# Gathering the rows of two expert tables alternately, head by head, in a fused two-block kernel

## The reference, cut to what matters

```python
def block(args):                 # 128 tokens: xb (128,1024), eb, gb (128,8,16)
    xb, eb, gb = args
    ub = u_tab[eb]
    act = _gelu(jnp.einsum('td,thkd->thk', xb, ub)) * gb
    vb = v_tab[eb]
    return jnp.einsum('thk,thkd->td', act, vb)
```

## Time and profile before

| what | value |
|---|---|
| median of three executions | 3803.32 us (3788.68 to 3813.45) |
| profiled execution: its own time | 3798.31 us |
| its span in the profile | 3796.5 us |
| TensorE clock granted, mean | 0.851 of full |
| first gather issued, last gather issued | 161.3 us, 1983.2 us |
| PE / VectorE / ScalarE / GpSimd busy | 70% / 54% / 21% / 49% of the span |

### The profile page before, as it was taken

One profiled execution on the slowest core, in us unless ns is written; L12 is line 12 of the kernel. 1 busy time (PEld: TensorE's weight loads), 2 busy tenths in 40 slices (PEclk: granted clock), 3 DMA queues, 4 the chain that ended last, 5 costly groups with the idle time before them and its releaser, 6 DMA issues.

```text
span 3796.5 us, 37057 instructions
## 1 busy us (share of the span) xinstructions
PE 2674.6 (70%) x14128; PEld 1994.0 (53%) x14128; DVE 2038.2 (54%) x4133; ACT 802.5 (21%) x1515; POOL 1860.8 (49%) x1389
## 2 busy tenths in 40 slices
PE   6521887207862277542776888888889998998999
PEld 3421444004431144211224777777789997777887
DVE  6599867888678877588443534544220103532010
ACT  2100111001110011111113322332332322443231
POOL 0166656775567756488761322222354543125463
PEclk8755999558886599776998987998999999999999
DMA  5388889897899879999991210000223332012332
GB/s 173 138 310 299 288 276 338 306 341 261 298 314 344 314 264 333 343 336 336 353 345 28 67 28 1 1 1 1 56 73 91 88 90 59 26 45 78 95 95 78
DMA packets 417970, 693.79 MB, mean 183 GB/s; under 512 B 35784, under 2 KB 280691, under 8 KB 417667
## 3 DMA queue, kind: packets, MB, share of 16 engines
q0 software_dynamic: 147456, 536.94, 39.7%
q1 hardware_dynamic: 270339, 154.50, 14.1%
HBM read 689.26 MB, written 2.10 MB: 182 GB/s over the span
## 4 chain that ended last, share of the span: by engine, by line
PE 51%; DVE 16%; POOL 12%; DMA 11%; issue 6%; ACT 3%; SPq 1%; DVEq 0%; ACTq 0%; POOLq 0%
PE PS L1601 25%; POOL ring L608 12%; DMA ring<-in_peer_v,eidx 7%; PE PS L775 7%; DMA ring<-in_peer_u,eidx 3%; DVE ring L1308 3%; PE PS L754 2%; PE PS L1502 1%; PE PS L1511 1%; PE PS L660 1%; PE PS L1508 1%; DVE W L1182 1%; PE PS L1611 1%; DVE X L1323 1%; PE PS L1623 1%
## 5 line engine op out<-in xcount | busy, mean ns | idle before, releaser
L608 POOL DMA_INDIRECT ring<-in_peer_u,eidx x512 | 630.7, 1232 | 409.1 <-DVE eidx L1285 175.9
L608 POOL DMA_INDIRECT ring<-in_peer_v,eidx x512 | 588.9, 1150 | 355.2 <-PE PS L775 215.4
L1601 PE MATMUL PS<-held_uH,GW 128*128 128x264 f32 (+1 forms) x3008 | 668.3, 316 | 35.4 <-POOL BIG_value L2128 31.3
L1308 DVE CUSTOM_DVE_ANT_0 ring<-ring,hn 128x1024 f32<-128x1024 f32 x512 | 615.7, 1224 | 117.9 <-DMA ring<-in_peer_u,eidx 110.8
L775 PE MATMUL PS<-ring,dg 128*128 128x512 f32 x1024 | 534.9, 662 | 168.7 <-DMA ring<-in_peer_v,eidx 164.4
L2114 POOL TENSOR_TENSOR GW<-held_wr,GW 128x1024 fp32r<-128x1024 f32 x178 | 428.9, 2411 | 449.5 <-ACT GW L1891 449.5
L1601 PEld LDWEIGHTS PS<-held_uH,GW 128*128 128x128 f32 x3008 | 504.2, 193 | 79.9 <-issue 34.1
L1601 PE MATMUL PS<-BIG_value,GW 128*128 128x264 f32 (+1 forms) x1504 | 448.1, 313 | 0.0
L775 PEld LDWEIGHTS PS<-ring,dg 128*128 128x128 f32 x1024 | 198.0, 208 | 460.8 <-DMA ring<-in_peer_v,eidx 281.3
L1323 DVE SCALAR_TENSOR_TENSOR X<-ring,gact,X 128x1024 f32<-128x1024 f32 x256 | 328.7, 1284 | 179.8 <-DMA ring<-in_peer_v,eidx 176.0
L1601 PE MATMUL PS<-hid,GW 128*128 128x264 f32 (+1 forms) x2304 | 368.6, 322 | 0.0
(11 more groups left out here) (465 smaller groups left out, 3581.1 us busy)
## 6 DMA issues: line engine op xcount, KB each, us to landing
held_wr<-in_w_ff SPq DMA_DIRECT2D x128, 512.0 KB, 4.1
wqr<-in_peer_wq SPq DMA_DIRECT2D x64, 512.0 KB, 8.0
held_wr<-in_w_in_ab SPq DMA_DIRECT2D x18, 512.0 KB, 3.7
ring<-in_peer_u,eidx POOLq DMA_INDIRECT x512, 6.2
ring<-in_peer_v,eidx POOLq DMA_INDIRECT x512, 6.0
BIG<-in_w_in SPq DMA_DIRECT2D x4, 1536.0 KB, 11.3
held_wr<-in_w_qkv_c SPq DMA_DIRECT2D x12, 512.0 KB, 3.9
w_out<-in_w_out SPq DMA_DIRECT2D x1, 4096.0 KB, 20.6
```

The lines of the kernel that those rows point to most:

```text
L608: e.indirect_dma_start(out=ring[:, i % RING, :], out_offset=None, in_=rows_u if k < HK else rows_v, in_offset=bass.IndirectOffsetOnAxis(ap ...
L1308: e.tensor_tensor_reduce(row, row, hn[:, :], 1.0, 0.0, ALU.mult, ALU.add, act[:, k:k + 1]).then_inc(*n.up(e_dot))
L1601: ins = e.matmul(bank[b + a][:, 0:w], (hi, lo)[w_][:, k * P:(k + 1) * P], (x_hi, x_lo)[x_][:, c0:c0 + w], start=(first and w_ == 0 and x_ ...
```

## The change

The list is written anew, and the consumers of the v rows are shared out otherwise.

- The u rows of block 0 come first, as before, with steps of front 0 alone. Then 110 of the 128 v rows of block 0 follow, with all 76 steps of front 1 spread evenly over them. `LAG = 18` is the number of v rows left.
- In blocks 1 to 3 each of the 128 places holds a pair: u row `k` of the block, and the v row that is next in turn, 18 v rows behind. After two of three pairs of blocks 1 and 2 a step of the next front follows (85 places for 76 steps). After every fourth pair of block 3 one step of the tails follows, but of tail 2 only the first; the other nine, `pproj` 3 and tail 3 come after the last v row. Eighteen v rows stand alone at the end.
- Gelu and the product with the gates are done for each head of 16 as its u rows end (8 of each per block instead of one).
- `on_vector`: in block 0, `k % 3 > 0` (85 rows) is added on VectorE; in blocks 1 to 3, `k % 3 == 1` (43 rows each). The others go to PE: 43 rows and 3 x 85 rows. It was 64 and 64 in every block.
- A diagonal is asked of ScalarE when fewer than three are outstanding, up to six v rows ahead. PE's first v row of a block waits until `experts_done` of the block before has read the banks.

```diff
+def on_vector(blk, k):
+    return k % 3 > 0 if blk == 0 else k % 3 == 1
+    def add_u(others):
+        blk, k = divmod(count["u"], HK)
+        while heads(blk) < k // TOPK + 1:
+            step(others)
+        if k == 0:
+            order.append(("begin", blk))
+            if blk == NB - 1:
+                order.append(("second",))
+        order.append(("u", blk, k))
+        count["u"] += 1
+        if k % TOPK == TOPK - 1:
+            order.append(("gelu", blk, k // TOPK))
+        if ended:
+            order.append(("end", ended.pop()))
+
+    def add_v():
+        m = count["v"]
+        for x in range(m, min(m + 2 * NDG, NB * HK)):
+            blk, k = divmod(x, HK)
+            head = x // TOPK
+            if x > m and (count["u"] < TOPK * (head + 1) or taken[("front", blk)] < FRONT_STEPS):
+                break
+            if head not in weighed:
+                order.append(("weigh", blk, k // TOPK))
+                weighed.add(head)
+            if not on_vector(blk, k) and x not in diagonals and len(diagonals) - count["pe"] < NDG:
+                order.append(("dg", blk, k))
+                diagonals.add(x)
+        blk, k = divmod(m, HK)
+        order.append(("v", blk, k))
+        count["v"] += 1
+        count["pe"] += not on_vector(blk, k)
+        if k == HK - 1:
+            ended.append(blk)
...
+    for k in range(HK):
+        add_u(fronts)
+        if k % 3 == 0:
+            step(fronts)
+    while taken[("front", 0)] < FRONT_STEPS:
         step(fronts)
+    fronts.append((("front", 1), FRONT_STEPS))
+    for k in range(HK - LAG):
+        add_v()
+        while fronts and taken.get(("front", 1), 0) * (HK - LAG) < FRONT_STEPS * (k + 1):
+            step(fronts)
...
+    for blk in range(1, NB):
+        for k in range(HK):
+            add_u(fronts)
+            if k == 0 and blk + 1 < NB:
+                fronts.append((("front", blk + 1), FRONT_STEPS))
+            add_v()
+            if blk == NB - 1:
+                if k % 4 == 3 and taken.get(("tail", 2), 0) < 1:
+                    step(late)
+            elif k % 3:
+                step(fronts)
+        while blk + 1 < NB and taken[("front", blk + 1)] < FRONT_STEPS:
+            step(fronts)
+    while count["v"] < NB * HK:
+        add_v()
+    order.append(("end", ended.pop()))
     while late:
         step(late)
     order += [("tail", 3)] * TAIL_STEPS
```

```diff
     def slot_free(e, i):
+        if i >= RING:
+            kind, blk, k = gathers[i - RING]
+            if kind == "u":
+                e.wait_ge(e_dot, HK * blk + k + 1)
+            elif on_vector(blk, k):
+                e.wait_ge(e_ax, ON_VECTOR.index((blk, k)) + 1)
+            else:
+                e.wait_ge(e_pv, ON_PE.index((blk, k)) + 1)
...
+    def diagonal(e, n, blk, k):
+        m = ON_PE.index((blk, k))
+        e.wait_ge(e_gact, (HK * blk + k) // TOPK + 1)
+        if m >= NDG:
+            e.wait_ge(e_pv, m - NDG + 1)
+        e.mul(dg[:, m % NDG, :], ident, gact[:, k:k + 1]).then_inc(*n.up(e_dg))
+
+    def gelu_scalar(e, n, blk, h):
+        at = slice(TOPK * h, TOPK * h + TOPK)
+        e.wait_ge(e_dot, HK * blk + TOPK * h + TOPK)
+        e.activation(gact[:, at], act[:, at], ACT.Gelu).then_inc(*n.up(e_gelu))
```

More of the change, by code:

```diff
@@ L122 @@
 NDG = 3
+LAG = 18
 NQ = 2
@@ L130 @@
 SETUP_STEPS = 7
+def on_vector(blk, k):
+    return k % 3 > 0 if blk == 0 else k % 3 == 1
+ON_PE = [(blk, k) for blk in range(NB) for k in range(HK) if not on_vector(blk, k)]
+ON_VECTOR = [(blk, k) for blk in range(NB) for k in range(HK) if on_vector(blk, k)]
 def first_order():
@@ L137, in first_order @@
     taken = {}
+    count = {"u": 0, "v": 0, "pe": 0}
+    weighed = set()
+    diagonals = set()
+    ended = []
     def step(streams):
@@ L149, in heads @@
         return (taken.get(("front", blk), 0) - 35) // 5
-    def experts(blk, others, pace):
-        while heads(blk) < 1:
+    def add_u(others):
+        blk, k = divmod(count["u"], HK)
+        while heads(blk) < k // TOPK + 1:
             step(others)
[L154 to L170, removed]
+        if k == 0:
[27 more added lines that the diff above has]
+            ended.append(blk)
     fronts = [(("front", 0), FRONT_STEPS)]
@@ L178, in first_order @@
             step(fronts)
-    while taken[("front", 0)] < 13:
-        step(fronts)
[L181 to L185, removed]
+    for k in range(HK):
[3 more added lines that the diff above has]
+    while taken[("front", 0)] < FRONT_STEPS:
+        step(fronts)
+    fronts.append((("front", 1), FRONT_STEPS))
[3 more added lines that the diff above has]
+            step(fronts)
     late = []
@@ L586, in emit @@
     rows_v = ap["peer_v"].rearrange("l n d -> (l n) d")
+    gathers = [name for name in first_order() if name[0] in ("u", "v")]
+    place = {name: i for i, name in enumerate(gathers)}
     def slot_free(e, i):
[L590 to L599, removed]
-    def first_pool(e):
[L602 to L611, removed]
+        if i >= RING:
[6 more added lines that the diff above has]
+                e.wait_ge(e_pv, ON_PE.index((blk, k)) + 1)
+    def first_pool(e):
+        for i, (kind, blk, k) in enumerate(gathers):
+            if kind == "u" and k % TOPK == 0:
+                e.wait_ge(r_idx, NH * blk + k // TOPK + 1)
+            slot_free(e, i)
+            e.indirect_dma_start(
+                out=ring[:, i % RING, :], out_offset=None, in_=rows_u if kind == "u" else rows_v,
+                in_offset=bass.IndirectOffsetOnAxis(ap=eidx[:, blk % 2, k:k + 1], axis=0),
+            ).then_inc(d_r[i % RING], 16)
     def row_there(i):
@@ L768, in expert_sum @@
     def expert_sum(e, n, blk, k):
[L770 to L777, removed]
+        if on_vector(blk, k):
+            return
+        i, m = place["v", blk, k], ON_PE.index((blk, k))
+        first = m == 0 or ON_PE[m - 1][0] < blk
+        last = m == len(ON_PE) - 1 or ON_PE[m + 1][0] > blk
+        e.wait_ge(*row_there(i))
+        e.wait_ge(e_dg, m + 1)
+        if first and blk:
+            e.wait_ge(e_x, blk)
+        for c in range(2):
+            ins = e.matmul(bank[6 + c], dg[:, m % NDG, :], ring[:, i % RING, 512 * c:512 * c + 512], start=first, stop=last)
+        ins.then_inc(*n.up(e_pv))
     def meta_tensor(e, n):
@@ L1002, in first_scalar @@
                 keep_hn(e, n, name[1])
[L1003 to L1007, removed]
+            elif name[0] == "gelu":
+                gelu_scalar(e, n, *name[1:])
+            elif name[0] == "dg":
+                diagonal(e, n, *name[1:])
             elif name[0] == "second":
@@ L1326, in experts_done @@
     def experts_done(e, n, blk):
-        e.wait_ge(e_pv, 64 * (blk + 1))
+        e.wait_ge(e_pv, sum(b <= blk for b, _ in ON_PE))
         e.wait_ge(*n.now(e_ax))
```

18 lines of the change are left out of this document (9 added, 9 removed).

## The result

The changed kernel took 3922.38 us (median of four, 3921.76 to 3926.53) against 3804.48 for the kernel before: ratio 1.0317, 95% interval 1.0282 to 1.0352. It is 3.2% slower; I had forecast no change (3800) and a range up to 3870.

What follows compares the result with a forecast made beforehand. It took VectorE (block 0's u rows) and PE with the ring (v rows beside fronts) as bounds; new stages 1796 against 1827.8 us, -32, plus 31 for the tail, gave 3800 us, range 3735 to 3870.

Steps and rivals of the forecast that it cites:

- What bounds the kernel now: Gather part: VectorE holds block 0's u rows, PE together with the ring the v rows beside a front; memory 1.50 us a row.
- Block 0, u rows, 230: Block 0's u rows: front 1's seven light steps leave this stage, so 232.4 us becomes 230.
- Block 0, 110 v rows, 268, and 27 at the end: Block 0's v rows with all of front 1: VectorE decides, 268 us; the 18 rows left over take 27 at the end.
- Blocks 1 and 2, 425 each: Pairs of blocks 1 and 2: memory bounds, 22 us of waits for PE remain; 425 us each, gaining 45 and 31.
- the bytes' bound: Block 1: 143.9 MB at 357 GB/s give a lower bound of 403 us.
- Block 3, 415, "the ring stood anyway": Block 3's pairs: early tail loads stop the ring as before, so 415 us instead of 412.2.
- Behind the last row, +31: After the last gathers: nine of tail 2's ten steps and `pproj` 3 become exposed, adding 31 us.
- The shared ring: Rival, blocks 0 to 2: PE's and VectorE's rows in one ring, each wait stops all; +50 +14, 3864 us; chance 0.15.
- GpSimd's lock: Rival, pairs of two blocks: VectorE's operations lengthen GpSimd's issues, 1.77 us a gather, 54 us more, 3854; chance 0.10.
- a mean over 1.3 us: Sign on GpSimd: a mean issue above 1.3 us would show the forecast wrong.

Runs made afterwards that it cites:

- e5: The changed kernel with PE multiplying only the first 512 of 1024 columns of its v rows, first and last of a block excepted: 3857.27 us, ratio 1.0165.
- e12: The changed kernel with all v rows of block 3 but the first on VectorE: 3904.44 us, ratio 1.0268.
- e7: The changed kernel's new order with the old shares, every second v row on VectorE in all blocks: 3931.28 us, ratio 1.0360.
- e2: The changed kernel with seven ring slots instead of six, layer norm's gain and offset left out: 3824.66 us, ratio 1.0051.
- e4: The changed kernel with two v rows in three on VectorE in block 3 too: 3914.52 us, ratio 1.0291.

## Why the prediction was wrong

- *What bounds the kernel now.* Right for the v rows with a front beside them: PE and the ring. (I gave PE's share and clock there as 76 to 79% and 0.86 to 0.94; the earlier trace rows has 78 to 79% and 0.89 to 0.94. Nothing rests on it.) I read the ring as a buffer behind PE. It is a limit of its own: landing and hold of one slot, divided by the slots.
- *Block 0, u rows, 230.* Measured 239.0; the runs in the new order gave 230.4 to 238.5, so part of the 9 us is spread between executions. Small, and the cause of the rest was not looked for.
- *Block 0, 110 v rows, 268, and 27 at the end.* Near: 273.2 and 26.0. VectorE at 78% of the stage, I had 81%.
- *Blocks 1 and 2, 425 each.* This step failed. I wrote that PE gets a row every third gather, that the rows behind a query product halve and a third of the waits for PE would remain, 22 us. PE's part of the waits fell only from 74 to 52, and the waits for VectorE, which my sum put at nothing, rose from 18 to 52, because u rows now stand behind the front's steps on VectorE all through the block. Together the waits for slots rose from 93 to 104 us where I had 22. The mistake is in what I took for the measure: not how many rows PE has, but how long any row of the six is held, by PE or by an engine that has something else before it in the list. The last v stage before has three PE rows in every six gathers and runs at 1.46 us a gather, with 2.04 us on PE for a row. Of the bytes' bound that I used (403) the rate is confirmed: with seven slots the second halves of both blocks run at 351 and 349 GB/s, and the blocks take 437.8 and 434.9.
- *Block 3, 415, "the ring stood anyway".* Failed in the same way: 457.6. GpSimd's waits for slots were 25.4 and 4.7 us in the u rows and 25.1 in the v rows before, 55 in all; now they are 90.3 + 10.2 = 100.5. The 45 more are the stage's 45.4. The one long wait at the start (23.6) is 4 more than the old one; the rest is spread over the turns. Here PE's rows are nearly the whole of it, and the hold is what e5 and e12 took away: with half the product the second half ran at 192.8, with no row on PE at 196.9.
- *Behind the last row, +31.* Right: +29.2; the other runs with this tail and six slots gave +22 to +36. The chain on the trace is two products of the tail one behind the other, with the small product of `pproj` 3 between:

```profile
2092.44 15.70 PE L867 MATMUL PS<-w_out,W 128*128 128x512 f32 x32 [2.15 <-DVE W L1392]
...
2117.83 5.26 PE L849 MATMUL PS<-BIG,W 128*128 128x512 f32 x8 [0.46 <-ACT W L1016]
...
2124.91 14.00 PE L867 MATMUL PS<-w_out,W 128*128 128x512 f32 x32 [0.94 <-DVE W L1392]
```

- *The rivals.* The shared ring was the one that came, with its mechanism (PE's rows and VectorE's u rows in one ring, each wait stopping all), but at a price of 64 where 122 over my forecast were to be paid, as I had let it touch blocks 0 to 2 and not block 3. I gave it a chance of 0.15. GpSimd's lock did not come: the page's groups of the changed kernel show its issues shorter than before, 1.188 us for u rows and 1.121 for v rows, where they were 1.232 and 1.150. The sign that I had named for it, a mean over 1.3 us, did not appear.

```profile
L657 POOL DMA_INDIRECT ring<-in_peer_u,eidx x512 | 608.5, 1188 | 451.6 <-DVE eidx L1336 177.9
...
L657 POOL DMA_INDIRECT ring<-in_peer_v,eidx x512 | 573.7, 1121 | 448.8 <-PE PS L829 264.7
```

In e12, where VectorE has nearly all rows of block 3 and is busy 83% of its second half, they last 156.36 / 129 = 1.21 us and together with the 0.3 between them fill the stage; in the changed kernel, with VectorE busy 52% there, it is 142.44 / 128 = 1.11. So GpSimd is close behind the memory as a bound, at about the number of the old u rows. By the exclusive lock of the Trainium skill (SBUF — State Buffer, "SBUF: two separate sides") the second of two operations that share the port pair waits for the whole of the first. The traces agree only in that the mean issue is 0.1 us longer beside the busier VectorE; no run shows whether the lock applies to an indirect DMA's issue.

What stays open: how much time the lower clock costs (2.81 us a row in the mean against 2.04), as the fillers brought a load of their own; how much of e7's missing gain is the longer hold; and the 10 to 13 us by which blocks 1 and 2 with seven slots still stand over my 425, where GpSimd still waits 38.4 us for dot products in block 1 of e2.

## What to carry to other kernels

With a ring of gathers issued in order, write down for each slot landing time plus hold, and divide by the number of slots: that quotient has to stay under the memory's time for a row. The hold is not only the consumer's time for the row, but also whatever stands before the row in that engine's part of the list. Putting a slow consumer's rows evenly among the others lowers the load of that consumer, but it lets its hold, and the front's steps on the other engine, touch the rows of all stages. A seventh slot was worth 98 us in the new order and about 40 in the old, going back to the old order 107; and a stage without a front, as block 3, shows soonest whether an order pays.

## What the runs showed of the hardware that I had not expected

In the mean a v row took PE 2.04 us in the last stage of the kernel before, with 64 rows in 191.7 us and a granted clock of 0.95, and 2.81 us in the second half of block 3 of the changed kernel, with 42 rows in 207.5 us and a clock of 0.78; single rows took 1.98 and up to 3.78. With fewer rows it went on: 3.30 us at 0.68 in e7, 3.66 at 0.62 in e4. The fewer rows PE had in a stage, the longer each of them took. One extra product behind each row brought the clock to 0.89, two to 0.97, without a gain in the whole.
